# The first block's out projection in three rounded terms, with the second norm taken row tile by row tile inside it

## What is computed

```python
def _mix_out(P, o_att, o_dn, w_out, o_norm_g):
    gate = jax.nn.silu(P['dz'].astype(jnp.float32)).reshape(B, L, DN_HEADS, DN_DIM)
    dn = (_rms(o_dn, o_norm_g) * gate).reshape(B, L, DN_CH).astype(o_att.dtype)
    cat = jnp.concatenate([_fourier(P['f']), o_att, dn], axis=-1)
    return cat @ w_out

def _mlp(h, w1, w2):
    u = jnp.maximum(h @ w1, 0.0)
    return (u * u) @ w2
...
    x = x + g1 * _mix_out(P, o_att, o_dn, lp['w_out'], lp['o_norm'])
    x = x + g2 * _mlp(_rms(x, lp['norm2']) * (1 + sc2) + sh2, lp['w_ff1'], lp['w_ff2'])
```

## Time and profile before

| | us |
|---|---|
| median of three runs | 1537.96 |
| the runs | 1540.37, 1535.28, 1537.96 |
| the profiled execution | 1535.46 |
| its span (first to last instruction) | 1533.4 |
| PE, DVE, ACT, POOL busy | 1454.3 (95%), 900.1 (59%), 698.8 (46%), 44.7 (3%) |
| out projection (line 2324), first to last product | 324.94 to 352.41 |
| first product of the first block's MLP (line 733) | 367.51 |

### The profile page before, as it was taken

How to read it: one execution, slowest core, us unless ns; L and a number is a source line. 1 busy time by engine, 2 the same in 40 slices (tenths; PEclk the granted TensorE clock), 3 DMA queues, 4 the chain that set the end, 5 groups by cost and what they waited for, 6 DMA issues and landing times. The chain is left out here.

```text
span 1533.4 us, 25756 instructions
## 1 busy us (share of the span) xinstructions
PE 1454.3 (95%) x10597; PEld 1185.9 (77%) x10597; DVE 900.1 (59%) x1410; ACT 698.8 (46%) x1184; POOL 44.7 (3%) x57
## 2 busy tenths in 40 slices
PE   4999989988999989999999999999999999999996
PEld 2557777656888869998887888878989887788885
DVE  1653343425656555577687656575557769656565
ACT  3232325433444434476743444454457664444443
POOL 0000530000000000000000000000000000000000
PEclk9999999999999999998999999999999999999998
DMA  9721651006455417432435655524733233855520
GB/s 347 272 105 37 231 202 38 2 1 219 171 186 191 138 38 218 165 111 71 150 111 202 241 190 216 186 68 132 200 110 126 96 111 110 329 178 205 196 78 27
DMA packets 121038, 230.14 MB, mean 150 GB/s; under 512 B 20080, under 2 KB 34672, under 8 KB 120176
## 3 DMA queue, kind: packets, MB, share of 16 engines
q1 hardware_dynamic: 118064, 223.80, 41.9%
q10 hardware_dynamic: 2880, 5.01, 1.0%
HBM read 227.76 MB, written 1.05 MB: 149 GB/s over the span
## 5 line engine op out<-in xcount | busy, mean ns | idle before, releaser
L772 DVE TENSOR_TENSOR work_rounded<-ring,work_rounded 128x1024 fp32r<-128x1024 f32 x208 | 240.9, 1221 | 88.3 <-ACT work_rounded L764 88.2
L733 PE MATMUL psum<-channels_rounded,work_rounded 128*128 128x512 f32 x768 | 273.4, 400 | 1.6 <-DVEq L1752 1.3
L746 PE MATMUL psum<-work_rounded 128*128 128x512 f32 x1152 | 266.5, 390 | 0.0
L993 PE MATMUL psum<-channels_rounded,ring_rounded 128*128 128x256 f32 x1728 | 249.1, 285 | 2.7 <-PEq L2935 1.5
L764 ACT ACTIVATE work_rounded<-ring 128x1024 fp32r<-128x1024 f32 x208 | 203.3, 1050 | 106.1 <-PE psum L746 102.6
L746 PEld LDWEIGHTS psum<-work_rounded 128*128 128x128 f32 x1152 | 214.6, 188 | 45.5
L993 PEld LDWEIGHTS psum<-channels_rounded,ring_rounded 128*128 128x128 f32 x1728 | 222.6, 191 | 9.1 <-issue 7.8
L735 PE MATMUL psum<-channels_rounded,work_rounded 128*128 128x256 f32 x768 | 216.2, 281 | 0.0
L733 PEld LDWEIGHTS psum<-channels_rounded,work_rounded 128*128 128x128 f32 x768 | 144.9, 189 | 38.1 <-issue 2.6
L735 PEld LDWEIGHTS psum<-channels_rounded,work_rounded 128*128 128x128 f32 x768 | 145.7, 190 | 0.8
L1498 DVE TENSOR_TENSOR ring_rounded<-ring,ring_rounded 128x1024 fp32r<-128x1024 f32 x80 | 94.1, 1197 | 29.5 <-ACT ring_rounded L1292 28.8
(11 more groups left out here) (366 smaller groups left out, 1997.8 us busy)
## 6 DMA issues: line engine op xcount, KB each, us to landing
ring<-in_w_in SPq DMA_DIRECT2D x20, 2048.0 KB, 8.1
ring<-in_w_ff SPq DMA_DIRECT2D x16, 2048.0 KB, 8.4
ring<-in_w_ff_in SPq DMA_DIRECT2D x16, 2048.0 KB, 8.0
ring<-in_w_ff_out SPq DMA_DIRECT2D x16, 2048.0 KB, 8.0
ring<-in_w_mod SPq DMA_DIRECT2D x12, 2048.0 KB, 9.0
ring<-in_w_out SPq DMA_DIRECT2D x6, 2048.0 KB, 8.3
ring<-in_w_in SPq DMA_DIRECT2D x8, 1024.0 KB, 5.7
ring<-in_w_up SPq DMA_DIRECT2D x4, 2048.0 KB, 8.0
```

The lines of the kernel that those rows point to most:

```text
L733: pe.matmul(v3(psum[:, 4 + m, :], SEQ), w1[0][:, k, m * P:(m + 1) * P], y_both[:, :, k, :], start=(k == 0), stop=False, skip_group_check=True)
L746: mm = pe.matmul(psum[:, 2 * t + n, :], h[ph][:, kq, t * P:(t + 1) * P], w2[pw][:, kq, n * 512:(n + 1) * 512], start=False, stop=False, sk ...
L772: dve.tensor_tensor(parts.low[i % 2][:, at], ring[:, SLOT * s + 1024 * c:SLOT * s + 1024 * (c + 1)], exact(parts.high[i % 2][:, at]), ALU. ...
L993: mm = pe.matmul(ps[:, at:at + SEQ], u[pw][:, k, col:col + P], y_parts[py][:, k, :], start=((k, n) == (0, 0)), stop=((k, n) == (KC - 1, 2)))
```

## The change

The out projection is formed in three rounded terms: 96 products of fp32r tiles. `cat_parts` are the high and the low of the mixers' output, `out_high` and `out_low` those of the projection's weights, in pieces of 128x1024 (`leaving_high` on ACT, `leaving_low` on DVE). The order changes on every engine:

- ACT makes seven of the eight weight highs inside the attention's steps and one behind it. It takes the power of the scan's sums itself (logarithm and exponential), copies the transposed outputs to their highs (`cat_rounded`), and makes the first unit of the MLP's highs ahead of the norm.
- PE puts the first eight gate-row products ahead of `catD`, forms tile 0 term by term (high x high, low channels x high, high x low weights) and tile 1 half by half, all three terms for each k. Between the halves of tile 1 it transposes the normed rows of tile 0 (`normed(0)`); behind them come the other eight gate-row products, three products of filler and the transposes of tile 1.
- The norm is taken per half row (`gathered`): ACT squares and sums 512 columns as soon as DVE has added a quarter, and takes the power; it scales the left half of the row, DVE the right half (`scaled_right`). Scale and shift are applied to 128 tokens at a time, four pieces on DVE (`shifted`) and four on ACT (`normed`).
- DVE's four lows of the MLP's first unit lie between the quarters: one behind the second, two ahead of the third, one behind it. The lows of tile 0's normed channels come ahead of the last quarter.
- POOL no longer takes part behind the scan.

The diff, cut and with less indentation; left out are the semaphores' declarations, the tiles' addresses and the bodies of `gated`, `scaled_right`, `shifted`, `low_quarter` and `cat_low`, which hold the operations that the text names:

```diff
-for n in ("catA0", "catA1", "catD", "g0_0", "g0_1", "g1_0", "g1_1"):
-    j.add(n, "act")
-for c in range(4):
-    j.add(f"h2T{c}", "dve")
+for name, by, bank in (("catA0", "dve", 4), ("catA1", "dve", 5), ("g0_0", "act", 6), ("g0_1", "act", 7),
+           ("catD", "dve", 3), ("h2T00", "dve", 4), ("h2T01", "act", 5), ("g1_0", "act", 6),
+           ("g1_1", "act", 7), ("h2T10", "dve", 4), ("h2T11", "act", 5)):
+    j.add(name, by, bank=bank)
...
+    out_low = [rounded(q.slot(f"out{hh}"), 512) for hh in range(2)]
+    def leaving(t, hh, k, wt, row, first=False, last=False):
+        if wt == 0:
+            weights = out_high[hh][k // 2][:, 512 * (k % 2):512 * (k % 2) + 512]
+        else:
+            weights = out_low[hh][:, k, :]
+        mm = pe.matmul(psum[:, 2 * t + hh, :], cat_parts[row][:, k, t * P:(t + 1) * P], weights,
+                       start=first, stop=last)
+        if last:
+            mm.then_inc(acc_full, 1)
+    def normed(t, filled=0):
+        for g, ready in enumerate((hat_left, hat_right)):
+            ps = w.open(f"h2T{t}{g}")
+            if g == 0:
+                dense(pe, ps, filled)
+            pe.wait_ge(ready, t + 1)
+            for i in range(4):
+                k = 4 * g + i
+                mm = pe.transpose(ps[:, i * P:(i + 1) * P], v3(x_hat2, D)[:, t, k * P:(k + 1) * P],
+                                  ident)
+            w.done(mm)
+    gate_rows_out(0)
     ps = w.open("catD")
     pe.wait_ge(dn_ready, 1)
     for i in range(4):
         k, t = i // 2, i % 2
         mm = pe.transpose(ps[:, i * P:(i + 1) * P], v3(o_all, 256)[:, t, k * P:(k + 1) * P], ident)
     w.done(mm)
+    pe.wait_ge(cat_high, 3)
+    for k0, k1 in ((0, 6), (6, 8)):
+        if k0:
+            pe.wait_ge(cat_high, 4)
         for hh in range(2):
+            for k in range(k0, k1):
+                pe.wait_ge(piece_high, 4 * hh + k // 2 + 1)
+                leaving(0, hh, k, 0, 0, first=(k == 0))
+    pe.wait_ge(cat_split, 1)
     w.after("catD")
-    for t in range(TT):
-        for hh in range(2):
-            u = landed(f"out{hh}")
-            for k in range(KC):
-                mm = pe.matmul(psum[:, 2 * t + hh, :], catT3[:, k, t * P:(t + 1) * P], u[:, k, :],
-                               start=(k == 0), stop=(k == KC - 1))
-            mm.then_inc(acc_full, 1)
...
+    for hh in range(2):
+        for k in range(KC):
+            leaving(0, hh, k, 0, 1)
+    for hh in range(2):
+        for k in range(KC):
+            pe.wait_ge(piece_low, 4 * hh + k // 2 + 1)
+            leaving(0, hh, k, 1, 0, last=(k == KC - 1))
+    for hh in range(2):
+        for k in range(KC):
+            leaving(1, hh, k, 0, 0, first=(k == 0))
+            leaving(1, hh, k, 0, 1)
+            leaving(1, hh, k, 1, 0, last=(k == KC - 1))
+        if hh == 0:
+            normed(0)
+    gate_rows_out(1)
+    normed(1, 3)
     mlp_open(pe)
...
+    def leaving_high(hh, c):
+        s = q.slot(f"out{hh}")
+        act.wait_ge(unit_in[s], q.landed(f"out{hh}"))
+        act.activation(out_high[hh][c], ring[:, SLOT * s + 1024 * c:SLOT * s + 1024 * (c + 1)],
+                       ACT.Copy).then_inc(piece_high, 1)
...
+        if n < 6:
+            leaving_high(n // 4, n % 4)
+        elif n == 7:
+            leaving_high(1, 2)
...
+    cat_rounded("catA0", 2)
+    act.wait_ge(sums_ready, 5)
+    step(act.activation(rs[:, 52:60], ss[:, 52:60], ACT.Ln, bias=eps, scale=1.0 / HD))
+    step.wait()
+    act.activation(rs[:, 52:60], rs[:, 52:60], ACT.Exp, scale=-0.5).then_inc(scales_ready, 1)
+    cat_rounded("catA1", 4)
+    act.activation(cat_parts[0][:, 0:2, :], catT3[:, 0:2, :], ACT.Copy).then_inc(cat_high, 1)
+    leaving_high(1, 3)
+    cat_rounded("catD", 6)
+    gate_rows_in(0)
     split_high(act, q, mlp, 0)
...
+    def gathered(t, hh):
+        act.wait_ge(x1_ready, 2 * t + hh + 1)
+        step(act.activation(square_out[:, 0:512], x3[:, t, 512 * hh:512 * (hh + 1)], ACT.Square,
+                            accum_out=ss[:, 60 + 2 * t + hh:61 + 2 * t + hh]))
+        step.wait()
+        one, arg = rs[:, 60 + t:61 + t], ln_arg[:, t:t + 1]
+        if hh == 0:
+            step(act.activation(arg, ss[:, 60 + 2 * t:61 + 2 * t], ACT.Identity, bias=eps,
+                                scale=1.0 / D))
+            return
+        step(act.activation(one, ss[:, 61 + 2 * t:62 + 2 * t], ACT.Ln, bias=arg, scale=1.0 / D))
+        step.wait()
+        act.activation(one, one, ACT.Exp, scale=-0.5).then_inc(scales_ready, 1)
+        act.wait_ge(scales_ready, 4 + t)
+        act.mul(v3(x_hat2, D)[:, t, 0:512], x3[:, t, 0:512], one).then_inc(hat_left, 1)
+    def normed(t):
+        ps = r.open(f"h2T{t}1")
+        for i in range(4):
+            k = 4 + i
+            last = act.activation(yT8[:, k, t * P:(t + 1) * P], ps[:, i * P:(i + 1) * P], ACT.Identity,
+                                  bias=modT3[:, 24 + k, 0:1], scale=a2[:, k:k + 1])
+            if i < 3:
+                step(last)
+        r.read(f"h2T{t}1", last)
+        r.settle()
+        for g in range(2):
+            if g == 0:
+                r.after(f"h2T{t}0")
+            act.activation(quarter(y_high, t, g), quarter(half_T, t, g), ACT.Copy).then_inc(y_in, 1)
+    gathered(0, 0)
+    gathered(0, 1)
+    gathered(1, 0)
+    normed(0)
+    gathered(1, 1)
+    gate_rows_in(1)
+    normed(1)
...
-    power(5, 52, 8, 1.0 / HD)
-    power(6, 60, 2, 1.0 / D)
...
+    leaving_low(0, 0)
     dve.wait_ge(scales_ready, 3)
     do(dve.tensor_tensor(v3(o_all, HD), v3(o_all, HD), spread(rs[:, 52:60], HD), ALU.mult))
     do(dve.tensor_tensor(v3(o_all, HD), v3(o_all, HD), same(row("o_norm"), 8), ALU.mult))
     dve.tensor_tensor(o_all, o_all, dz, ALU.mult).then_inc(dn_ready, 1)
...
+    cat_low("catA0", 2, 1)
+    cat_low("catA1", 4, 2)
+    dve.wait_ge(cat_high, 3)
+    dve.tensor_tensor(cat_parts[1][:, 0:2, :], catT3[:, 0:2, :], exact(cat_parts[0][:, 0:2, :]),
+                      ALU.subtract).then_inc(cat_split, 1)
+    cat_low("catD", 6, 4)
+    for c in range(1, 8):
+        leaving_low(c // 4, c % 4)
...
+    r.after("g0_1")
+    gated(0, 0, 0, 1)
+    gated(0, 0, 1, 2)
+    split_low(dve, q, mlp, 0, chunks=(0,))
+    scaled_right(0)
+    split_low(dve, q, mlp, 0, chunks=(1, 2))
+    gated(0, 1, 0, 3)
+    shifted(0)
+    split_low(dve, q, mlp, 0, chunks=(3,))
+    step(low_quarter(0, 0))
+    step(low_quarter(0, 1))
+    gated(0, 1, 1, 4)
+    scaled_right(1)
+    shifted(1)
+    r.settle()
+    low_quarter(1, 0).then_inc(y_split, 2)
+    low_quarter(1, 1).then_inc(y_split, 2)
```

145 lines of the change are left out of this document (65 added, 80 removed).

## The result

The changed kernel takes 1522.24 us (median of 5 runs, 1517.49 to 1527.25), the kernel before 1537.96 (1535.28 to 1540.37): the ratio is 0.9902, with a 95% interval of 0.9884 to 0.9920. That is 15.7 us less, about 1%, and the forecast was 1522.

What follows compares the result with a forecast made beforehand. TensorE bounds the kernel, and the MLP's start moves: 4.5 + 4.3 + 6.7 = 15.5 us earlier, giving 1520.0 us from the profiled run, 1522.5 from the median; forecast 1522 (chance 0.70), range 1516.5 to 1528.

Steps and rivals of the forecast that it cites:

- What bounds the kernel: Whole kernel: TensorE is busy nearly throughout; the MLP's start at 367.51 us moves, and everything behind follows as a block.
- Two of the signs named: Profile after: MLP's first product at 351 to 353 us; forecast wrong if the attention ends later than 314.5.
- The start of the projection: Before the out projection: eight gate rows move into TensorE's 3.11 us wait, so it starts at 320.4, 4.5 us earlier.
- The projection: Out projection: 96 rounded products at 0.230 us plus tile 0's transposes take 23.2 us, not 27.5; 4.3 us less.
- ScalarE's highs at nothing: Attention: seven weight highs of 1.05 us each on ScalarE fit into its steps and cost nothing.
- the case that the cover is gone: Attention: if ScalarE's seven highs were no longer hidden, up to 7.35 us; rival of a delayed attention, 1530 us, chance 0.04.
- The tail: From the projection's last product to the MLP's first: 8.35 us against 15.1, so 6.7 us less.
- the rule weighed there: Tail's 128-wide shifts: smaller pieces pay fixed time per instruction; page estimates 0.26 us each, forecast took 0.40.
- VectorE as the bound: During projection and tail: VectorE has 23.5 us of work in 24.7; rival, gain only 12.5 to 14.5 us, chance 0.13.
- The dip at the MLP: MLP's start: rival in which 2.8 us at half clock vanish, gaining 17 us in all, 1521 us, chance 0.08.
- The slower rival: Out projection: all 96 products at the low clock take 44.2 us, not 22.1; 1544.6 us, chance 0.03.
- The weights' loads: Loads released by the third and fourth quarter have some 7 us less in hand; costed at nothing.

Runs made afterwards that it cites:

- The gate rows' run: All sixteen gate-row products put back between the scan's transposes and the projection, against the changed kernel: stage 40.96 us, total 1527.41 us, 0.9943 of the kernel before.

## Why the prediction was right, step by step

**What bounds the kernel:** right. What was gained between the attention and the MLP arrived at the end: 16.75 us in the stage of the traces, 15.7 in the medians of the first timing and 16.7 in the second. The sum's 15.5 is 1.25 less than the stage's gain, 1.0 of it at the start of the projection. That the median came within 0.3 us of the 1522 is partly luck: the median of the kernel before alone moved from 1537.96 to 1540.61 between timings.

**Two of the signs named** came out, as they were written, on the wrong side: the attention ends at 318.4 and not by 314.5, and the MLP's first product comes at 354.74 and not at 351 to 353. They are absolute times, and the trace is 3.98 us late ahead of the stage, with more low stretches than the first trace of the kernel before; the second trace of the kernel before is late as well (its stage starts at 318.35 and not 315.01). Measured from the stage's start the MLP comes at 315.01 + 35.75 = 350.76 on the prediction's scale.

**The start of the projection:** forecast 4.5 us earlier, measured 9.93 - 4.40 = 5.53. The scan's output came 0.24 earlier (VectorE's last scaling ended 3.87 us behind the stage's start and not 4.11), without GpSimd's 1.64 in the chain. The rest lies in the scan's transposes: the first product followed 0.39 us behind their start, where the next row followed at 0.88 before and at 1.2 in the sum. About 0.3 of that is a reading: the sum took the row's modelled end for its successor's start. The other half microsecond is the clock, which the prediction let stay low to the end of the gate rows, and which was at 1.00. With a low stretch there, as in the second trace, the gain is 5.25. The gate rows' run says the same from the other side, 5.21.

**The projection:** forecast 23.2 us with tile 0's transposes, measured 23.13, at 0.23 us a product and with no wait for a low. The term was right in size, and the run in full f32 shows that it is the form that pays: 5.45 us, of which the 1.1 for the transposes that moved in had been taken off in the sum.

**ScalarE's highs at nothing:** right; the attention takes 68.47 us after 68.48. The price named for the case that the cover is gone, up to 7.35 us, is the highs' own time, and it leaves out a term. In the runs, one execution each, half as much again costs 0.3 us and twice as much 30.8: with the overrun came the low clock, which the prediction did not connect with the attention.

**The tail:** forecast 8.35 us (8.05 from the terms, and 0.3 in hand for late gate rows or slow shifts), measured 8.22. Four 128-wide shifts took 1.37 us on VectorE and 1.51 on ScalarE, forecast 1.6. On the rule weighed there: a shift is 0.34 us, so neither 0.54 (a shift of 256 columns costs the same per instruction) nor 0.27 (half). The Trainium skill, page "VectorE: DVE Perf Modes", section "The TRN2 errata — SBUF-src ops pay a fixed extra latency per instruction", comes to an estimated 0.26 for it; the measurement decides, and it lies 0.08 above. The page is right that narrow pieces don't get cheap in proportion: two of 128 columns cost 0.69 where one of 256 cost 0.540.

**VectorE as the bound:** it did not become that, but the margin is as thin as the sum said: 0.36 us ahead of the last quarter, 1.4 hidden of 2.5 added.

**The lows and the norm:** the two halves of the tail's term were not priced apart ahead of time. Undone one by one, the lows are worth 2.6 us and tile 0's early norm 3.5 (3.94 less the low stretch); with the gate rows' 5.2 and the form's 5.45 that makes 16.7, the whole gain, though such pieces need not add up.

**The dip at the MLP** stayed in the first trace (0.52 for 3.5 us) and was absent in the second, so that, as far as two traces tell, the rival in which it goes is a matter of the execution and not of the change. **The slower rival**, the projection at the low clock, did not come in any trace. **The weights' loads** cost next to nothing: ScalarE's highs of the MLP still wait for TensorE, 102.7 of their 106.1 us, as in the earlier trace rows; for loads they wait 3.4 us, and 2.9 before the change.

## What to carry to other kernels

Sum such a change over the one stretch between two points that it can't move, and read that stretch from the trace: it repeats to some tenths where whole executions differ by ten microseconds. Work put into an engine's waits is free until that engine ends later than the one it serves; measure the margin by adding work there, since the first overrun may cost a clock level and not its own length. Work that depends on nothing belongs into the wait itself, where here even a low clock moved what follows by half a microsecond at most.

## What the runs showed of the hardware

In the run with all highs done twice, waits of 0.28 and 0.15 us were followed by 75.1 us at 0.50, in which PE counts as busy for 72.51 of 75.00 us. With a filler ahead of every transposed probability, the same work ran at 1.00 and 22.2 us sooner. The Trainium skill, page "TensorE: Matmul & The Clock Gate", section "HAM oscillation — how this bites in real kernels", shows a kernel whose waits between pieces of work put TensorE back to its slow level, and restructures it so that TensorE stays warm. These runs agree in the direction only: the page's waits are for transfers and many times longer than the 0.43 us here. The same page, section "What's actually happening", says that "the default state is throttled, and activity releases the throttle"; here TensorE's work went on nearly without a gap for 75 us and the clock stayed low. One execution shows this, so how regularly the fall comes at that size is open.

The fall also comes and goes in unchanged code. The kernel before had none near 113 us in one trace and 3.4 us of it in the next, the changed kernel had some 65 us of low stretches ahead of its end in one trace and some 51 in the other. What decides it at a given place isn't settled here.
